# Residual products spread over the norms, high products first, at the boundaries between the calls of a two-block fp32 transformer

## The chip, the cores and the metric

One core of one Trainium2 chip runs the whole program in one launch. The metric is the device time in microseconds; a program's figure is the median of its runs.

## The reference

Two blocks of two layers each work on x, 256 tokens of 1024 channels, in fp32. The first block has attention with context and a Fourier mixer; the second has an RWKV-7 and an mLSTM mixer. What the change touches is the skeleton around them:

```python
# first block, each layer
x_mid = x + g1 * rmsnorm(mix, norm_post_mix[i])
hf = modulate(rmsnorm(x_mid, norm_pre_ffn[i]), sh2, sc2)
x = x_mid + g2 * rmsnorm(swiglu(hf, w_gate[i], w_up[i], w_down[i]), norm_post_ffn[i])
...
# second block, each layer
h = h + HALF * _swiglu(_rmsnorm(h, ffn1_norm[l]), ffn1_w_in[l], ffn1_w_out[l])
xn = _rmsnorm(h, mix_norm[l])
z = xn @ w_in[l]
...
h = h + u @ w_out[l]
h = h + HALF * _swiglu(_rmsnorm(h, ffn2_norm[l]), ffn2_w_in[l], ffn2_w_out[l])
```

`rmsnorm` is x / sqrt(mean(x²) + 1e-6) times a gain, and `modulate` is h(1 + scale) + shift.

## The kernel before

Channels lie on the 128 partitions, so x is 8 blocks (`KD`) of 128 x 256. Weights stream from memory through two-slot rings (`ring_a`, `ring_d`), 1 MB or 0.5 MB at a time. The large products are exact to about fp32 in three reduced-precision (fp32r) products: each operand is split into a high part (a rounding copy) and a low part (the rest), and hi·hi + hi·lo + lo·hi are summed in PSUM (`split_product`, lines 2030 to 2032).

Each engine has its own program, and semaphores join them. There is no scheduler: the order on each engine is the order of the code.

- **TensorE** (`block.tensor`): a norm is `norm_sums` (column sums of the squares, line 2000), `norm_tokens` (line 2009) and `norm_spread` (the inverse root onto all partitions, line 2018). A feed-forward call (`ffn`, seven of them, calls 0 to 6, 22 tiles each) alternates a gate and up tile (`wide_gate_up`, lines 2048 and 2050) with a down tile. In `wide_gate_up` the high and the low part of h stand side by side in `h_parts`, so that one 512-column matmul takes both. Calls 3 to 6 accumulate 2x into the down banks first (lines 2098 to 2103): eight *residual products* of the constant `twice` with a block of x, each two matmul records since it is plain fp32. The sum of 2x and the down product, halved, is the new x.
- **ScalarE**: the norms' squares (`norm`, `norm_squares`, lines 638 and 644), the row copy (662) and the square root (669), the weights' high parts (`round_a`, line 679; `round_d`; t_hi, line 1012), the high parts of h (`round_h`, line 694, with modulation 697 and 698), the evictions and the activations.
- **VectorE**: the reciprocal (`inverse`, 1277), the scaling by the norm (`norm_split`, 1349 and 1351), the weights' low parts (`rest_a`, 1330; `rest_t`, 1608), the halving into x (`half_to_x`, 1587), the addition onto x (1291).
- **GpSimd**: the eight low parts of h (`rest_h`, line 563), and most of the mixer's weight low parts (585).

A boundary between calls is then: squares, sums, row copy, token sums, root, reciprocal, spread, scaling, high parts, low parts, first tile. In TensorE's code all residual products stand between the spread and the first tile, and the first tile's block k waits for the low part of block k (`split_here`). At the first block's second layer ScalarE's `norm` rounds the first weights ahead of the squares of x. The other calls in question are ffn1, mixer and ffn2 of the second block's two layers.

## Time and profile before

| | us |
|---|---|
| median of 3 runs (2487.69 to 2493.08) | 2489.09 |
| the profiled execution's own time | 2488.33 |
| its span in the profile | 2485.8 |
| TensorE busy | 2369.6 (95%) |
| VectorE busy | 1449.3 (58%) |
| ScalarE busy | 1047.2 (42%) |
| GpSimd busy | 319.3 (13%) |

The mean granted clock of TensorE is 0.98 of 2.4 GHz. TensorE's busy time counts a matmul as busy at either clock, so a stretch at 1.2 GHz does not show as idle. The chain that ended last goes through TensorE for 82% of the span. The other engines' busy times are therefore of interest only where TensorE waits for them, and what follows looks there.

### The profile page before, as it was taken

To read this page: it belongs to the slowest core of one execution; us is meant where nothing else is said; L and a number is where in the kernel's file an instruction comes from. 1 tells how busy PE (TensorE), PEld (TensorE's weight loads), DVE (VectorE), ACT (ScalarE), POOL (GpSimd) and SP (SyncE) were. 2 spreads that over 40 slices of the span, in tenths; PEclk is the share of its full clock that TensorE was granted. 3 is DMA by queue.
4 is the path that set the end of the run, shared out by engine and by line. 5 is a ranking of instruction groups with operands and counts; after the bars stand their busy time and mean duration, and the time that the engine had idled before them with its cause. 6 is when DMAs were issued, how large, how long until landed. Compare 5 with 4: busy or idle time off the path is not lost.

```text
span 2485.8 us, 47529 instructions
## 1 busy us (share of the span) xinstructions
PE 2369.6 (95%) x19164; PEld 2095.1 (84%) x19164; DVE 1449.3 (58%) x2314; ACT 1047.2 (42%) x1666; POOL 319.3 (13%) x263
## 2 busy tenths in 40 slices
PE   7988999999998799999999999999999999999998
PEld 3755899999985599879988888899899888988997
DVE  1053266656625276676667765566666668555665
ACT  3154454454335343343346434433433355435333
POOL 0000000000000000010014435300100125336000
PEclk9999999999999899999999999999999999999999
DMA  6255454544425454355433223654455232124542
GB/s 267 71 198 216 178 191 176 189 169 176 169 85 219 154 203 179 150 178 190 177 106 123 81 72 125 220 189 177 154 189 190 102 138 100 69 87 178 201 179 102
DMA packets 65512, 392.51 MB, mean 158 GB/s; under 512 B 7264, under 2 KB 7392, under 8 KB 28000
## 3 DMA queue, kind: packets, MB, share of 16 engines
q1 hardware_dynamic: 64224, 383.81, 42.3%
q10 hardware_dynamic: 864, 5.16, 0.5%
q8 instruction: 104, 1.70, 0.3%
...
HBM read 389.46 MB, written 1.05 MB: 157 GB/s over the span
## 4 chain that ended last, share of the span: by engine, by line
PE 82%; DVE 4%; POOL 4%; issue 4%; ACT 3%; DMA 2%; POOLq 0%; SPq 0%; DVEq 0%; ACTq 0%
PE ps L2048 19%; PE ps L2030 11%; PE ps L2031 11%; PE ps L2032 11%; PE ps L2050 10%; PE ps L2139 6%; POOL t_lo L585 3%; PE ps L2154 2%; PE ps L2453 2%; DMA ring_a<-in_wa 2%; PE ps L2594 1%; POOL h_parts L563 1%; PE ps L2000 1%; PE ps L1977 1%; PE ps L2169 1%
## 5 line engine op out<-in xcount | busy, mean ns | idle before, releaser
L2048 PE MATMUL ps<-h_parts,w_hi 128*128 128x512 f32 x2080 | 742.1, 399 | 4.8 <-DVE mod L1258 2.9
L2050 PE MATMUL ps<-h_parts,w_lo 128*128 128x256 f32 x2080 | 584.9, 281 | 0.0
L2048 PEld LDWEIGHTS ps<-h_parts,w_hi 128*128 128x128 f32 x2080 | 391.9, 188 | 96.7 <-DVE mod L1258 3.2
L2050 PEld LDWEIGHTS ps<-h_parts,w_lo 128*128 128x128 f32 x2080 | 394.1, 189 | 0.1
L1330 DVE TENSOR_TENSOR w_lo<-ring_a,w_hi 128x1024 fp32r<-128x1024 f32 x308 | 366.5, 1232 | 24.7 <-ACT w_hi L679 24.5
L2030 PE MATMUL ps<-hid_hi,d_hi 128*128 128x256 f32 x1232 | 349.0, 283 | 0.0
L2031 PE MATMUL ps<-hid_lo,d_hi 128*128 128x256 f32 x1232 | 348.8, 283 | 0.0
L2032 PE MATMUL ps<-hid_hi,d_lo 128*128 128x256 f32 x1232 | 348.6, 283 | 0.0
L711 ACT ACTIVATE sg<-sg 128x256 f32<-128x256 f32 x130 | 54.3, 418 | 655.5 <-DVE sg L1366 655.5
L679 ACT CAST w_hi<-ring_a 128x1024 fp32r<-128x1024 f32 x308 | 305.6, 1040 | 12.3 <-DMA ring_a<-in_wa 12.3
L2030 PE MATMUL ps<-h_parts,t_hi 128*128 128x256 f32 x880 | 260.8, 296 | 17.4 <-POOL t_lo L585 10.6
L1366 DVE TENSOR_REDUCE sg<-ps 128x256 f32<-128x512 f32 x130 | 89.9, 692 | 302.4 <-PE ps L2050 302.4
L2031 PE MATMUL ps<-h_parts,t_hi 128*128 128x256 f32 x880 | 252.8, 287 | 0.0
L2032 PE MATMUL ps<-h_parts,t_lo 128*128 128x256 f32 x880 | 252.5, 287 | 0.0
L563 POOL TENSOR_TENSOR h_parts<-nsq,h_parts 128x256 fp32r<-128x256 f32 x72 | 61.4, 876 | 1435.1 <-ACT h_parts L698 849.3
L2030 PEld LDWEIGHTS ps<-hid_hi,d_hi 128*128 128x128 f32 x1232 | 234.2, 190 | 6.0
L2032 PEld LDWEIGHTS ps<-hid_hi,d_lo 128*128 128x128 f32 x1232 | 234.6, 190 | 0.0
L2031 PEld LDWEIGHTS ps<-hid_lo,d_hi 128*128 128x128 f32 x1232 | 234.5, 190 | 0.0
L585 POOL TENSOR_TENSOR t_lo<-ring_a,t_hi 128x512 fp32r<-128x512 f32 x120 | 172.7, 1463 | 314.6 <-ACT t_hi L1012 314.6
L1337 DVE TENSOR_TENSOR d_lo<-ring_d,d_hi 128x1024 fp32r<-128x1024 f32 x154 | 190.1, 1235 | 11.5 <-ACT d_hi L687 8.9
L2030 PEld LDWEIGHTS ps<-h_parts,t_hi 128*128 128x128 f32 x880 | 172.2, 196 | 25.9 <-issue 13.6
L2031 PEld LDWEIGHTS ps<-h_parts,t_hi 128*128 128x128 f32 x880 | 173.0, 197 | 0.1
...
## 6 DMA issues: line engine op xcount, KB each, us to landing
...
c<-in_c ACTq DMA_DIRECT2D x1, 1175.0 KB, 10.8
...
```

Of the source, the lines that this page charges most:

```text
L563: nc.gpsimd.tensor_tensor(h_lo[:, k, :], nsq[:, k, :], h_hi[:, k, :].bitcast(F32), ALU.subtract)\
L585: nc.gpsimd.tensor_tensor(t_lo[:, t % 2, k], ring_a[:, c % 2, t % 2, k], t_hi[:, t % 2, k].bitcast(F32), ALU.subtract).then_inc(done, 1)
L679: nc.scalar.copy(w_hi[:, f % 2, part], ring_a[:, c % 2, part]).then_inc(hi_a, 1)
L1330: ins = nc.vector.tensor_tensor(w_lo[:, f % 2, part], ring_a[:, c % 2, part], w_hi[:, f % 2, part].bitcast(F32), ALU.subtract)
L1337: nc.vector.tensor_tensor(d_lo[:, f % 2], ring_d[:, d % 2], d_hi[:, f % 2].bitcast(F32), ALU.subtract)\
L1366: nc.vector.reduce_sum(sg[:, f % 2, :], both_parts(bank), AX_X).then_inc(gate_summed, 1)
L2030: nc.tensor.matmul(out, hi, to_hi, start=start, stop=False, skip_group_check=True)
L2031: nc.tensor.matmul(out, hi, to_lo, start=False, stop=False, skip_group_check=True)
L2032: return nc.tensor.matmul(out, lo, to_hi, start=False, stop=stop, skip_group_check=True)
L2048: nc.tensor.matmul(out, w_hi[:, f % 2, part, k, :], h_parts[:, k], start=(k == 0), stop=False, skip_group_check=True)
L2050: mm = nc.tensor.matmul(out[:, 1, :], w_lo[:, f % 2, part, k, :], h_hi[:, k, :], start=False, stop=(k == KD - 1), skip_group_check=True)
L2139: mm = nc.tensor.matmul(ps[:, 4 + p % 2, 0:cols.stop - cols.start], ring_a[:, slot, i % 2, k, :], h[:, k, cols], start=(k == 0), stop=(k = ...
```

## The change

It does six things.

1. The eight residual products leave the place ahead of the first tile. `norm_residual` puts them between the pieces of the sums, before the token sums, before the spread and behind it, and `ffn(..., last=...)` puts some between tile 0 and tile 1. Each waits for its own piece of x.
2. The first gate and up tile of calls 2 to 6 (`first_gate_up`) and the mixer's first weight tile (`first_tile`) make all products with h's high part first, then those with its low part. The 512-column matmul becomes two of 256 columns.
3. Of h's low parts GpSimd makes five, and VectorE three behind its scaling (both `rest_h`). This holds for calls 2 to 6 and both mixers.
4. In the first block's second layer the squares of the first norm go between the evictions of the projection, the squares of x ahead of the first weights' rounding, which is cut in two, and VectorE writes the modulated h itself (`norm_modulated`) where ScalarE wrote it before.
5. VectorE makes the low part of the first weights earlier (before `half_to_x`) ahead of call 5, and tile 0's low part before `half_to_x` in the mixers.
6. Two turns of the modulation's rows stand ahead of the norm's sums instead of around them.

```diff
...
-                for k in range(KD):
+                for k in range(KD if sid < SHARED else POOL_REST):
                     pool.wait_ge(hh_ready, sid * KD + k + 1)
+                    if sid == SHARED:
+                        pool.wait_ge(h_whole, k + 1)
                     nc.gpsimd.tensor_tensor(h_lo[:, k, :], nsq[:, k, :], h_hi[:, k, :].bitcast(F32), ALU.subtract)\
...
-                        nc.scalar.activation(nsq[:, k, :], hn[:, k, :], ACT.Identity, scale=gains(k), bias=shift(k))
+                        if sid < SHARED:
...
                 modulated = lambda which: (gain_of(l, 2, which), shift_of(l, 3, which))
                 for j in range(KD):
                     empty(f"out1{l}", j, lat[:, j, :])
-                    if l == 0 and j % 2:
+                    if j % 2:
                         if j == 1:
-                            nc.scalar.activation(warm[:, 2:3], const("one"), ACT.Sqrt)
-                        act.wait_ge(proj_free, tile0["out10"] + j + 1)
+                            at = n_id[("post_mix", l, 0)]
+                            nc.scalar.activation(warm[:, at:at + 1], const("one"), ACT.Sqrt)
+                        act.wait_ge(proj_free, tile0[f"out1{l}"] + j + 1)
                         norm_squares(lat, None, [j // 2])
...
                 else:
-                    act.wait_ge(proj_free, tile0[f"out1{l}"] + KD)
-                    norm(("post_mix", l, 0), lat)
-                    g0, g1 = fill(f"M{l}0")
-                    ada(g0)
-                    norm(("pre_ffn", l, 0), x[:, :, :], 2, onto=("post_mix", l, 0), also=lambda: ada(g1))
+                    norm_rows(("post_mix", l, 0))
+                    norm_root(("post_mix", l, 0))
+                    for g in fill(f"M{l}0"):
+                        ada(g)
+                    norm_squares(x[:, :, :], ("post_mix", l, 0))
+                    norm_rows(("pre_ffn", l, 0))
+                    round_a(2, 0, parts=[0])
+                    norm_root(("pre_ffn", l, 0))
+                    round_a(2, 0, parts=[1])
                     round_h(split_id[("pre_ffn", l, 0)], modulated(0))
                     ffn(2)
...
 
-            def norm_split(key, src, call=None, gains=None):
-
-                n, sid = n_id[key], split_id[key]
+            def rest_h(key):
+
+                sid = split_id[key]
+                for k in range(POOL_REST, KD):
+                    dve.wait_ge(hh_ready, sid * KD + k + 1)
+                    nc.vector.tensor_tensor(h_lo[:, k, :], nsq[:, k, :], h_hi[:, k, :].bitcast(F32), ALU.subtract)\
+                        .then_inc(hl_tail if k < KD - 1 else norm_out, 1)
+
+            def norm_split(key, src, call, gains):
+
                 if call is not None:
                     rest_a(call, 0)
                 inverse(key)
-                dve.wait_ge(norm_all, n + 1)
+                dve.wait_ge(norm_all, n_id[key] + 1)
                 for k in range(KD):
-                    if gains is None:
-                        ins = nc.vector.tensor_tensor(hn[:, k, :], src[:, k, :], rstd_of(key), ALU.mult)
-                    else:
-                        ins = nc.vector.scalar_tensor_tensor(nsq[:, k, :], src[:, k, :], gains(k), rstd_of(key),
-                                                             ALU.mult, ALU.mult)
-                    ins.then_inc(v_ready, 1)
+                    nc.vector.scalar_tensor_tensor(nsq[:, k, :], src[:, k, :], gains(k), rstd_of(key),
+                                                   ALU.mult, ALU.mult).then_inc(v_ready, 1)
+                rest_h(key)
+
+            def norm_modulated(key, src, call, gains, shift):
+
+                inverse(key)
+                rest_a(call, 0)
+                dve.wait_ge(norm_all, n_id[key] + 1)
+                for k in range(KD + 1):
+                    if k < KD:
+                        nc.vector.tensor_tensor(hn[:, k, :], src[:, k, :], rstd_of(key), ALU.mult).then_inc(v_ready, 1)
+                    if k:
+                        dve.wait_ge(v_ready, split_id[key] * KD + k)
+                        nc.vector.tensor_scalar(nsq[:, k - 1, :], hn[:, k - 1, :], gains(k - 1), shift(k - 1),
+                                                ALU.mult, ALU.add).then_inc(h_whole, 1)
+                dve.wait_ge(h_whole, KD)
+                rest_h(key)
 
             def ffn(call, beside=None):
...
             dve.wait_ge(norm_out, n_id[("post_ffn", 1, 0)] + 1)
             for l in range(LAYERS):
-                norm_split(("ffn1", l, 0), x, 3 + 2 * l, per_channel("ffn1", l))
+                norm_split(("ffn1", l, 0), x, None if l else 3, per_channel("ffn1", l))
                 ffn(3 + 2 * l)
-                half_to_x(("mix", l, 0))
                 p0 = l * NT2
 
                 def rest_t(t):
@@ -1609,6 +1641,7 @@
                                                 t_hi[:, t % 2, k].bitcast(F32), ALU.subtract).then_inc(done, 1)
 
                 rest_t(0)
+                half_to_x(("mix", l, 0))
...
                 ffn(4 + 2 * l)
+                if l + 1 < LAYERS:
+                    rest_a(5 + 2 * l, 0)
                 half_to_x(("ffn1", l + 1, 0) if l + 1 < LAYERS else ("final", 0, 0))
...
+            def norm_sums(key, before=None):
...
                 for k in range(KD):
+                    if before is not None and k % (KD // PIECES) == 0:
+                        before(k * PIECES // KD)
                     strip = slice(k % STRIPS * STRIP, (k % STRIPS + 1) * STRIP)
                     pe.wait_ge(norm_sq, PIECES * n + k * PIECES // KD + 1)
...
                 norm_tokens(key)
                 norm_spread(key)
 
+            def residual(call, ns):
+
+                for n in ns:
+                    piece = n * PIECES // KD
+                    if call > 3:
+                        pe.wait_ge(resid, PIECES * (3 * ((call - 3) // 2) + (call - 3) % 2 * 2 - 1) + piece + 1)
+                    elif piece < PIECES - 1:
+                        pe.wait_ge(onto_part, (PIECES - 1) * onto_id[("post_ffn", 1, 0)] + piece + 1)
+                    else:
+                        pe.wait_ge(norm_out, n_id[("post_ffn", 1, 0)] + 1)
+                    nc.tensor.matmul(ps[:, n // 2, n % 2 * T:n % 2 * T + T], const("twice"), x[:, n, :],
+                                     start=(n % 2 == 0), stop=False, skip_group_check=True)
+
+            def norm_residual(key, call, pieces, tokens, spread, after):
+
+                norm_sums(key, lambda i: residual(call, pieces[i]))
+                residual(call, tokens)
+                norm_tokens(key)
+                residual(call, spread)
+                norm_spread(key)
+                residual(call, after)
+
             def split_product(out, parts, start, stop):
 
                 hi, lo, to_hi, to_lo = parts
@@ -2033,16 +2092,41 @@
 
             def split_here(key, k):
 
-                if k < KD - 1:
-                    pe.wait_ge(hl_ready, split_id[key] * (KD - 1) + k + 1)
+                sid = split_id[key]
+                if k == KD - 1:
+                    pe.wait_ge(norm_out, n_id[key] + 1)
+                elif sid < SHARED or k < POOL_REST:
+                    pe.wait_ge(hl_ready, pool_rests(sid) + k + 1)
                 else:
-                    pe.wait_ge(norm_out, n_id[key] + 1)
+                    pe.wait_ge(hl_tail, (sid - SHARED) * (KD - 1 - POOL_REST) + k - POOL_REST + 1)
+
+            def hi_here(key, k):
+                pe.wait_ge(hh_ready, split_id[key] * KD + k + 1)
+
+            def first_gate_up(key):
+
+                def out(part, half):
+                    return ps[:, gate_up_bank(0) + part, half * T:half * T + T]
+
+                for k in range(KD):
+                    hi_here(key, k)
+                    for part in range(2):
+                        nc.tensor.matmul(out(part, 0), w_hi[:, 0, part, k, :], h_hi[:, k, :], start=(k == 0),
+                                         stop=False, skip_group_check=True)
+                        nc.tensor.matmul(out(part, 1), w_lo[:, 0, part, k, :], h_hi[:, k, :], start=False,
+                                         stop=False, skip_group_check=True)
+                for k in range(KD):
+                    split_here(key, k)
+                    for part in range(2):
+                        mm = nc.tensor.matmul(out(part, 1), w_hi[:, 0, part, k, :], h_lo[:, k, :], start=False,
+                                              stop=(k == KD - 1), skip_group_check=True)
+                return mm
 
             def wide_gate_up(key, f):
 
+                if f == 0:
+                    return first_gate_up(key)
                 for k in range(KD):
-                    if f == 0:
-                        split_here(key, k)
                     for part in range(2):
                         out = ps[:, gate_up_bank(f) + part, :].rearrange("p (a t) -> p a t", t=T)
...
 
-                if call >= 3:
-
-                    pe.wait_ge(norm_out, n_id[("post_ffn", 1, 0)] + 1)
-                    pe.wait_ge(resid, PIECES * (3 * ((call - 3) // 2) + (call - 3) % 2 * 2))
-                    for n in range(KD):
-                        nc.tensor.matmul(ps[:, n // 2, n % 2 * T:n % 2 * T + T], const("twice"), x[:, n, :],
-                                         start=(n % 2 == 0), stop=False, skip_group_check=True)
                 gate_up(0)
+                residual(call, last)
                 gate_up(1)
                 if call == 1:
...
             for l in range(LAYERS):
-                norm(("ffn1", l, 0))
-                ffn(3 + 2 * l, ("ffn1", l, 0))
+                if l == 0:
+                    norm_residual(("ffn1", l, 0), 3, [(), (0, 1), (2, 3), (4, 5)], (6,), (7,), ())
+                    ffn(3, ("ffn1", l, 0))
+                else:
+                    norm_residual(("ffn1", l, 0), 5, [(), (), (), ()], (0,), (1,), (2, 3, 4))
+                    ffn(5, ("ffn1", l, 0), last=(5, 6, 7))
                 norm(("mix", l, 0))
...
                     wait(pe, t_free, p0 + t - 1, i, 4)
+                    if t == 0:
+                        first_tile(ps[:, bank, 0:T]).then_inc(t_done, 1)
+                        return
                     for k in range(KD):
-                        if t == 0:
-                            split_here(("mix", l, 0), k)
...
                     mm.then_inc(b_done, 1)
-                norm(("ffn2", l, 0))
-                ffn(4 + 2 * l, ("ffn2", l, 0))
+                norm_residual(("ffn2", l, 0), 4 + 2 * l, [(), (), (), (0, 1)], (2,), (3,), (4, 5))
+                ffn(4 + 2 * l, ("ffn2", l, 0), last=(6, 7))
```

The mixer's `first_tile` follows `first_gate_up` with one weight tile in place of two: 16 products with the high part, then 8 with the low part. On TensorE, between the norm in front of call 3 and its first tile (`x,c` is the residual product, `nsq,c` a sum of squares, `c,nrt` the token sums, `c,nst` the spread), there stood before:

```order
L2000 MATMUL ps<-nsq,c 32x256 x8
L2009 MATMUL ps<-c,nrt 128x1 x2
L2018 MATMUL ps<-c,nst 128x128 x2
L2102 MATMUL ps<-x,c 128x256 x8
L2048 MATMUL ps<-h_parts,w_hi 128x512
L2050 MATMUL ps<-h_parts,w_lo 128x256
```

and now stand:

```order
L2037 MATMUL ps<-nsq,c 32x256 x2
L2074 MATMUL ps<-x,c 128x256 x2
L2037 MATMUL ps<-nsq,c 32x256 x2
L2074 MATMUL ps<-x,c 128x256 x2
L2037 MATMUL ps<-nsq,c 32x256 x2
L2074 MATMUL ps<-x,c 128x256 x2
L2037 MATMUL ps<-nsq,c 32x256 x2
L2074 MATMUL ps<-x,c 128x256
L2046 MATMUL ps<-c,nrt 128x1 x2
L2074 MATMUL ps<-x,c 128x256
L2055 MATMUL ps<-c,nst 128x128 x2
L2114 MATMUL ps<-h_parts,w_hi 128x256
```

All eight residual products have moved ahead of the spread. For calls 4 and 6 the places are: two before the last piece of sums, one before the token sums, one before the spread, two behind it, two between tile 0 and tile 1; for call 5 one, one, three and three.

On VectorE, ahead of call 2 in the first block's second layer (`work` is the normalised x in one place and the mix in the other, `mod` the modulation), there stood before:

```order
L1291 TENSOR_TENSOR x<-x,work 128x512 x2
L1258 TENSOR_TENSOR mod<-ps,vec 128x4
L1330 TENSOR_TENSOR w_lo<-ring_a,w_hi 128x1024 x2
L1277 RECIPROCAL nst<-nst 128x2
L1349 TENSOR_TENSOR work<-x,ps 128x256 x8
L1258 TENSOR_TENSOR mod<-ps,vec 128x4
L1269 SCALAR_TENSOR_TENSOR gain<-mod,vec 128x16
L1330 TENSOR_TENSOR w_lo<-ring_a,w_hi 128x1024 x2
```

and now stand:

```order
L1292 RECIPROCAL nst<-nst 128x2
L1345 TENSOR_TENSOR w_lo<-ring_a,w_hi 128x1024 x2
L1381 TENSOR_TENSOR work<-x,ps 128x256 x2
L1384 TENSOR_SCALAR nsq<-work,gain,mod 128x256
...
L1381 TENSOR_TENSOR work<-x,ps 128x256
L1384 TENSOR_SCALAR nsq<-work,gain,mod 128x256 x2
L1360 TENSOR_TENSOR h_parts<-nsq,h_parts 128x256 x3
L1284 SCALAR_TENSOR_TENSOR gain<-mod,vec 128x16
L1345 TENSOR_TENSOR w_lo<-ring_a,w_hi 128x1024 x2
```

The first weights' low pair has moved behind the reciprocal, each of the eight scalings has a modulation behind it, and three low parts of h stand ahead of the second weights' low pair.

## Rows read from the trace of the kernel before

**Rows 1.** The page, first part: busy us, share of the span, records.
```profile
PE 2369.6 (95%) x19164; PEld 2095.1 (84%) x19164; DVE 1449.3 (58%) x2314; ACT 1047.2 (42%) x1666; POOL 319.3 (13%) x263
```

**Rows 2.** Windows (stretch, length, busy us and records per engine, clock, DMA share, GB/s).
```profile
837.00:871.00 34.00, 19.30 (x121) 13.26 (x122) 14.46 (x30) 21.66 (x40) 5.88 (x8) 0.75 0.41 155
1260.00:1278.00 18.00, 14.84 (x89) 12.99 (x88) 11.44 (x21) 8.15 (x17) 6.47 (x8) 0.72 0.17 60
1570.00:1585.00 15.00, 13.28 (x80) 10.38 (x79) 12.02 (x17) 8.54 (x15) 8.07 (x9) 1.00 0.55 211
```

**Rows 3.** Timeline ahead of call 2, A (start, us, engine, line, operation, idle before, releaser).
```profile
839.58 2.09 PE L2000 MATMUL ps<-nsq,c 128*32 128x256 f32 x16 [2.59 <-ACT nsq L638]
...
848.46 1.29 DVE L1291 TENSOR_TENSOR x<-x,work 128x512 f32<-128x512 f32 x2
...
850.07 1.99 ACT L679 CAST w_hi<-ring_a 128x1024 fp32r<-128x1024 f32 x2 [4.45 <-DMA ring_a<-in_wa]
851.97 2.19 ACT L638 ACTIVATE nsq<-x 128x512 f32<-128x512 f32 x4
...
857.62 1.22 PE L2018 MATMUL ps<-c,nst 128*128 128x128 f32 x4 [0.55 <-DVE nst L1277]
...
870.77 0.50 PE L2048 MATMUL ps<-h_parts,w_hi 128*128 128x512 f32 x1 [1.31 <-DVE w_lo L1330]
```

**Rows 4.** Groups by line and form (busy us, mean ns, idle before, releaser).
```profile
L1330 DVE TENSOR_TENSOR w_lo<-ring_a,w_hi 128x1024 fp32r<-128x1024 f32 x308 | 366.5, 1232 | 24.7 <-ACT w_hi L679 24.5
...
L563 POOL TENSOR_TENSOR h_parts<-nsq,h_parts 128x256 fp32r<-128x256 f32 x72 | 61.4, 876 | 1435.1 <-ACT h_parts L698 849.3 <-ACT h_parts L694 585.7
...
L1631 DVE TENSOR_SCALAR work<-work,vec 128x256 f32<-128x256 f32 x8 | 2.3, 349 | 0.1
```

**Rows 5.** Timeline ahead of call 3, B.
```profile
1061.33 1.07 PE L2000 MATMUL ps<-nsq,c 128*32 128x256 f32 x4 [3.10 <-ACT nsq L638]
1062.62 1.07 PE L2000 MATMUL ps<-nsq,c 128*32 128x256 f32 x4 [0.22 <-ACT nsq L638]
...
1067.71 1.22 PE L2018 MATMUL ps<-c,nst 128*128 128x128 f32 x4 [0.55 <-DVE nst L1277]
...
1078.71 0.39 PE L2048 MATMUL ps<-h_parts,w_hi 128*128 128x512 f32 x1
...
1068.97 3.22 DVE L1351 SCALAR_TENSOR_TENSOR nsq<-x,vec,ps 128x256 f32<-128x256 f32 x8 [1.32 <-PE ps L2018]
1073.62 3.33 DVE L1330 TENSOR_TENSOR w_lo<-ring_a,w_hi 128x1024 fp32r<-128x1024 f32 x2 [1.42 <-ACT w_hi L679]
...
1069.49 3.15 ACT L694 CAST h_parts<-nsq 128x256 fp32r<-128x256 f32 x8 [2.03 <-DVE nsq L1351]
...
1069.98 7.56 POOL L563 TENSOR_TENSOR h_parts<-nsq,h_parts 128x256 fp32r<-128x256 f32 x8 [5.28 <-ACT h_parts L694]
```

**Rows 6.** Timeline ahead of layer 0's mixer, C.
```profile
1263.79 0.71 PE L2018 MATMUL ps<-c,nst 128*128 128x128 f32 x4 [0.62 <-DVE nst L1277]
...
1269.18 2.23 DVE L1608 TENSOR_TENSOR t_lo<-ring_a,t_hi 128x512 fp32r<-128x512 f32 x2 [1.42 <-ACT t_hi L1012]
...
1277.09 0.39 ACT L1028 ACTIVATE work<-ps 128x256 f32<-128x256 f32 x1 [2.61 <-PE ps L2032]
```

**Rows 7.** Timeline of TensorE ahead of call 4, D.
```profile
1571.77 0.63 PE L2000 MATMUL ps<-nsq,c 128*32 128x256 f32 x4 [0.46 <-ACT nsq L638]
...
1574.02 0.71 PE L2018 MATMUL ps<-c,nst 128*128 128x128 f32 x4 [0.55 <-DVE nst L1277]
1574.57 3.62 PE L2102 MATMUL ps<-x,c 128*128 128x256 f32 x16
...
1584.18 0.40 PE L2048 MATMUL ps<-h_parts,w_hi 128*128 128x512 f32 x1
```

**Rows 8.** Timeline of TensorE ahead of call 5, E.
```profile
1770.66 1.22 PE L2018 MATMUL ps<-c,nst 128*128 128x128 f32 x4 [1.83 <-DVE nst L1277]
...
1781.76 0.39 PE L2048 MATMUL ps<-h_parts,w_hi 128*128 128x512 f32 x1
```

36 lines of the change are left out of this document (27 added, 9 removed).

## The prediction

> **What bounds the kernel now.** I read the page first: TensorE is busy 95% of the span, 2369.6 us over 19164 matmul records [rows 1]. That is 0.124 us a record, so I take 0.12 us for a 256-column matmul in a stream. Time can only come off where TensorE does not stream, and the change touches seven such places, the boundaries between calls. I name them in order of time: A (before call 2), B (call 3), C (mixer of layer 0), D (call 4), E (call 5), F (mixer of layer 1), G (call 6). The windows around them show what is there [rows 2]: in 34 us around A TensorE is busy 19.3 us at a granted clock of 0.75 of full speed, around C 14.8 of 18 us at 0.72, around D 13.3 of 15 us at 1.00. Many of these boundaries cost twice: holes, and work at 1.2 GHz behind the holes. Then I read each boundary in the timeline. I measure from the end of the norm's spread (the scale factors' matmul) to the start of the next dense tile.
>
> In B the spread ends at 1067.71 + 1.22 = 1068.93, and the second gate and up tile starts at 1078.71, 9.8 us later. Between them, counted from the spread's end: VectorE scales to 3.3 us, ScalarE rounds the high parts from 0.6 to 3.7 us, GpSimd makes the eight low parts from 1.05 to 8.6 us, and VectorE needs 4.7 to 8.0 us for the next weights' low part [rows 5]. So GpSimd is the limiter, and the residual products that stand ahead of the first tile (16 records, 3.62 us at full clock, 0.45 us each of eight [rows 7]) lie mostly beside it. In D the same distance is 1584.18 - 1574.73 = 9.45 us [rows 7], in E 1781.76 - 1771.88 = 9.9 us [rows 8]. In C tile 0 and tile 1 are over at 1277.09, 12.6 us behind the spread's end at 1264.50 [rows 6].
>
> **The common part of the change.** High products no longer wait for GpSimd: they start with the first rounded block at 1.0 us and follow it. 32 of them at 0.12 us take 3.9 us, to 4.9 us; 16 low products add 1.9, to 6.8 us. GpSimd keeps five blocks; at 0.88 us a block (the mean of [rows 4]) they end at 5.4 us. VectorE takes three behind its scaling at 3.3 us. No row shows such a block on VectorE: the low bound is 0.35 us (a 128x256 tensor-scalar [rows 4]), the high bound is 1.2 us, GpSimd's mean block 0.88 plus 0.35 of its own. I take 0.7, between them, because the w_lo pair beside GpSimd took 3.33 us [rows 5] where two at 1.232 us would take 2.46 [rows 4]: the two engines do hold each other up. So VectorE is free at 3.3 + 2.1 = 5.4, and the w_lo pair of the next weights, now alone, ends at 5.4 + 2.4 = 7.8 us. That sets the second tile; the bounds give 6.8 (the low products) and 9.3. The Trainium skill, "SBUF — State Buffer", section "SBUF: two separate sides", says that such a pair of instructions takes an exclusive lock for its whole length, so that one engine fully waits. By it the three blocks of 0.35 us could stand behind two whole GpSimd blocks, 3.3 + 1.05 + 1.76 + 2.4 = 8.5 us, 0.7 worse than my value at each place, about 5 us over all seven; without any contention it would be 6.8 us, up to 7 us better over all. The stretched pair agrees with the direction.
>
> **Boundaries D and G.** Two residuals stand before the last piece of the sums, where TensorE now waits 0.46 us [rows 7]; they take 0.9, so the norm slips 0.45, say 0.5 us. The next two fit into the waits of about 0.5 us for the row copy and the reciprocal (0.55 in [rows 7]). Two more fit ahead of the first rounded block, and the last two between tile 0 (6.8) and 7.8. Gain 9.45 - 7.8 - 0.5 = **1.15 us each, 2.3 together** (bounds -0.4 and 1.8 each). G repeats D.
>
> **Boundary E.** The weights' low pair moves ahead of the half-scaling of x, and the reciprocal stops waiting for it: it delays the spread by 1.83 - 0.55 = 1.3 us now [rows 7, 8], and the spread itself runs 0.5 us longer at half clock (1.22 against 0.71). I take 1.8. The new price is that the half-scaling starts 1 us later; the square roots hide that. Behind the spread come three residuals (1.35 us, 0.35 beyond the hole) and three more behind the first tile: 6.8 + 0.3 + 1.3 = 8.4, which is later than 7.8 and sets the time. Gain 1.8 + 9.9 - 8.4 = **3.3 us** (2 to 4).
>
> **Boundary B.** Here the residuals are a risk. The sums wait for x, piece by piece (3.10 us before the first [rows 5]), and the clock is at half: four records take 1.07 us against 0.63 [rows 5, 7]. Two residuals, four records, cost 0.9 us at full clock and 1.7 at half, three times; the pieces' sums start 1.3 us apart now, with waits of 0.22 us between. So TensorE sets the norm. At half clock until the third pair its end slips by 3.2 us and gets back 0.9, because the steps behind the sums then run at full clock (the spread alone 0.71 us against 1.22 [rows 5, 7]): 2.3 later. If the denser work brings the clock back after the first pair it ends 0.5 later. The common part gives 9.8 - 7.8 = 2.0. So the boundary is worth between -0.3 and +1.5; I take **0.5 us**.
>
> **Boundaries C and F.** The same split, with one weight tile: 16 high products, 8 low ones. Tile 1's first low half would be ready when VectorE is free (5.4) plus half of a pair of 0.65 us, 6.05. At full clock its 24 records end at 8.95, 3.6 us earlier than 12.6; if the clock stays at half as long as now, 1.3 us earlier. I take **2.8 us each, 5.6 together**, between these and nearer the first, since TensorE has fewer gaps there. VectorE's t_lo pair (2.23 us beside GpSimd [rows 6]) loses its companion, which is the reason it is not later. Moving tile 0's low part ahead of the half-scaling costs nothing: the reciprocal is waited for by ScalarE's root either way. F repeats C.
>
> **Boundary A** has three parts. (1) The squares of the first norm are made between the projection's evictions, their table load too. Sums end at 841.67 now; only the last piece (0.63 of square, 0.4 of sums) is left behind the last eviction at 837.4, so they end at 838.6: 3.1 us. (2) The squares of x wait behind the weights' rounding, which waits for its DMA until 850.07; they start at 851.97, though x was complete at 849.75 [rows 3]. Now they go first, as x comes, and the rounding goes into the norm's waits. With x complete 3.1 us earlier, at 846.65: squares done at 847.3, sums 848.0, root 849.8, spread 851.2 at half clock instead of 858.84. The price is on VectorE: the low pair now stands between reciprocal and scaling, to 852.5. (3) ScalarE makes one rounding a block in place of two; VectorE makes the whole part with a tensor-scalar of 0.35 us [rows 4] behind each scaling. A scaling takes 3.22 / 8 = 0.40 us in B [rows 5]: eight rounds of 0.75, to 858.5 (1.1 each if every round waits for GpSimd). Then three low blocks and the gains (1.8 us, to 860.3) and the low pair, 2.4: 862.7, or 863.0 with the waits between. The second tile started at 870.77 [rows 3]. Gain **7.8 us** (bounds 5.3 with each block held up and half clock, 9 without). No DMA is late: the weights' load is released by the ada products, which also come 3.1 us earlier.
>
> **The sum**: 7.8 + 0.5 + 2.8 + 1.15 + 3.3 + 2.8 + 1.15 = 19.5 us. All tiles behind a boundary are TensorE's own time, so I let nothing be given back. The profiled execution took 2488.33 us (span 2485.8) and would take 2468.8. The median of the runs shown is 0.8 us above it; I say 2469.
>
> **Rivals.** (a) *Holes that are no holes*: residuals delay the norms by their full length, as when ScalarE's and VectorE's replies come sooner than a residual ends. Against it stand the waits of 0.46 to 0.55 us beside 0.45. It would take 1.3 us each from D and G, 0.9 from E, 2 from B, 5.5 in all: 2474. (b) *The half clock stays* through the new, denser starts: C and F give 1.3 each, B -0.3, A 5.3, E 2.3, D and G as forecast: 12.2 in all, 2476. For it speaks that before it stayed down through tile 0 and into tile 1 at C. (c) *VectorE becomes the chain*: its three blocks take 1.7 us each behind GpSimd. Then the second tile starts at 3.3 + 5.1 + 2.4 = 10.8: D and G lose 1.85 each, B 2.3, E gains 0.9, C and F lose 0.2 each, A keeps 4: 1.5 us slower, 2490. (d) *Slower: new drops of the clock.* The drops of before fall on stretches where TensorE waits anyway. If the changed rhythm brought a drop of some 10 us (as long as the half-clock stretch that I see behind C) onto dense tiles, half of it is lost, 5.1 us. With one at each of seven boundaries that is 36 - 19.5 = 16 slower, 2505; it decides from four such drops on. Against it: D has none, and the holes get shorter. The Trainium skill, "TensorE: Matmul & The Clock Gate", section "Part 1: The HAM clock gate (the "warmup" mystery)", says that an idle array loses its clock and a busy one gets it back, which speaks against (d).
>
> **How the numbers follow.** Forecast 0.74 (own range 2463 to 2476, from the bounds of A, B and the common part), (a) 0.09, (b) 0.10, (c) 0.04, (d) 0.03. The range is 2462 to 2480: it takes in (a) and (b) and a few us for the spread of the median. A measurement here tells 0.2%, 5 us, from no change. The first three cases are faster by more, 0.93; (c) is within it, 0.04; (d) slower, 0.03.
>
> **What would show it.** Right: the residual line's records spread over the norms; the second tile 7.5 to 8.5 us behind each spread; the spread at A 7.6 us earlier, its second tile 7.8; VectorE's three low blocks at 0.5 to 0.9 us. Wrong: a clock below 0.9 around D or G; sums at B that end more than 2 us later; w_lo of the second weights past 9 us. If the boundaries shrink and the span doesn't, something behind them gave the time back.

## The result, and the profile after

The changed kernel takes 2470.15 us (median of 4 runs, 2469.92 to 2472.8), the kernel before beside it 2491.09 us (4 runs, 2487.69 to 2493.79). The ratio is 0.9918, 95% interval 0.9904 to 0.9932. The forecast was 2469. When the changed kernel ran again beside the experiments below it took 2467.91 us, ratio 0.9919 (0.99 to 0.9939).

The page's first part, of the changed kernel's profiled execution (2472.8 us, span 2471.0):

```profile
PE 2367.2 (96%) x19244; PEld 2093.0 (85%) x19244; DVE 1455.8 (59%) x2343; ACT 1043.9 (42%) x1657; POOL 299.5 (12%) x242
```

Against [rows 1] TensorE is busy 2.4 us less with 80 records more: 512-column matmuls were cut in two. The time came out of its idle time. The windows around A, C and D (columns as in [rows 2], each window moved with its place):

```profile
833.00:867.00 34.00, 27.37 (x174) 20.73 (x173) 19.96 (x41) 17.16 (x29) 3.67 (x5) 0.85 0.51 186
1254.00:1272.00 18.00, 15.69 (x118) 14.13 (x117) 14.39 (x28) 9.87 (x20) 3.69 (x5) 0.91 0.16 58
1561.00:1576.00 15.00, 14.28 (x100) 11.23 (x98) 12.33 (x20) 8.72 (x16) 6.02 (x6) 1.00 0.63 240
```

Against [rows 2], TensorE is busy 8 us more of the 34 at A and its clock is 0.85 instead of 0.75; at C the clock is 0.91 instead of 0.72. GpSimd's eight blocks are five. D stays at full clock. (A window at A that starts with the last eviction, at 840.24, has the same 27.37 us and 0.85.)

The timeline at A, for TensorE, ScalarE, VectorE and GpSimd in turn:

```profile
840.13 1.82 PE L2037 MATMUL ps<-nsq,c 128*32 128x256 f32 x16
...
853.22 0.71 PE L2055 MATMUL ps<-c,nst 128*128 128x128 f32 x4 [0.77 <-DVE nst L1292]
...
866.20 0.50 PE L2132 MATMUL ps<-h_parts,w_hi 128*128 128x512 f32 x1 [0.98 <-DVE w_lo L1345]
...
847.86 1.15 ACT L667 ACTIVATE nsq<-x 128x512 f32<-128x512 f32 x2
...
856.00 0.41 DVE L1384 TENSOR_SCALAR nsq<-work,gain,mod 128x256 f32<-128x256 f32 x1
856.32 0.41 DVE L1381 TENSOR_TENSOR work<-x,ps 128x256 f32<-128x256 f32 x1
856.65 0.78 DVE L1384 TENSOR_SCALAR nsq<-work,gain,mod 128x256 f32<-128x256 f32 x1
...
862.57 1.10 DVE L1360 TENSOR_TENSOR h_parts<-nsq,h_parts 128x256 fp32r<-128x256 f32 x3
...
856.56 0.73 POOL L572 TENSOR_TENSOR h_parts<-nsq,h_parts 128x256 fp32r<-128x256 f32 x1 [356.76 <-DVE nsq L1384]
```

The first norm's sums come directly behind the last eviction (they end at 841.95; the last eviction started at 840.24). The squares of x (L667) start at 847.86, before x is complete. The spread ends at 853.93 (858.84 before), and the second gate and up tile starts at 866.20 (870.77 before [rows 3]). The starts alone hide one thing: the last eviction ahead of A, in code the change does not touch, was 3.2 us later in this profile (837.03 before). Measured from there, the gain at A is 7.8 us. The section on the hardware tells what is known of the 3.2 us.

The timeline at B (TensorE, VectorE, GpSimd):

```profile
1056.84 1.07 PE L2037 MATMUL ps<-nsq,c 128*32 128x256 f32 x4 [3.10 <-ACT nsq L647]
1057.84 2.07 PE L2074 MATMUL ps<-x,c 128*128 128x256 f32 x4
1059.84 0.62 PE L2037 MATMUL ps<-nsq,c 128*32 128x256 f32 x4
...
1065.33 0.71 PE L2055 MATMUL ps<-c,nst 128*128 128x128 f32 x4
...
1073.77 0.50 PE L2132 MATMUL ps<-h_parts,w_hi 128*128 128x512 f32 x1 [0.65 <-DVE w_lo L1345]
...
1069.22 2.22 DVE L1360 TENSOR_TENSOR h_parts<-nsq,h_parts 128x256 fp32r<-128x256 f32 x3
1071.37 2.35 DVE L1345 TENSOR_TENSOR w_lo<-ring_a,w_hi 128x1024 fp32r<-128x1024 f32 x2
...
1067.09 3.73 POOL L572 TENSOR_TENSOR h_parts<-nsq,h_parts 128x256 fp32r<-128x256 f32 x5 [6.87 <-ACT h_parts L703]
```

Two residuals (L2074) took 2.07 us at half clock; behind them the clock was full. The norm, from the first sums to the spread's end, became 1.6 us longer (9.20 against 7.60 from [rows 5]), and the second tile starts 7.7 us behind the spread instead of 9.8: 0.46 us gained.

When the changed kernel ran again, its profile showed B otherwise (TensorE):

```profile
1049.82 2.08 PE L2074 MATMUL ps<-x,c 128*128 128x256 f32 x4
...
1052.83 2.08 PE L2074 MATMUL ps<-x,c 128*128 128x256 f32 x4
...
1058.85 0.71 PE L2055 MATMUL ps<-c,nst 128*128 128x128 f32 x4
```

Four residuals ran at half clock there, the norm took 10.73 us, and B lost 1.05 us.

At C, one of TensorE's high products and ScalarE's second eviction:

```profile
1261.55 0.41 PE L2449 MATMUL ps<-h_parts,t_lo 128*128 128x256 f32 x1
...
1268.95 0.39 ACT L1043 ACTIVATE work<-ps 128x256 f32<-128x256 f32 x1 [1.98 <-PE ps L2091]
```

The spread ends at 1259.76, so the two tiles are over 9.2 us behind it, not 12.6 [rows 6]: 3.4 us. F shows the same 3.4.

The timeline at D (TensorE, VectorE, GpSimd):

```profile
1565.72 0.71 PE L2055 MATMUL ps<-c,nst 128*128 128x128 f32 x4
...
1573.03 1.22 PE L2121 MATMUL ps<-h_parts,w_hi 128*128 128x256 f32 x8 [0.47 <-POOL h_parts L572]
1574.08 1.02 PE L2074 MATMUL ps<-x,c 128*128 128x256 f32 x4
1574.75 0.58 PE L2132 MATMUL ps<-h_parts,w_hi 128*128 128x512 f32 x1
...
1569.61 1.09 DVE L1360 TENSOR_TENSOR h_parts<-nsq,h_parts 128x256 fp32r<-128x256 f32 x3
1571.11 2.94 DVE L1345 TENSOR_TENSOR w_lo<-ring_a,w_hi 128x1024 fp32r<-128x1024 f32 x2 [0.42 <-ACT w_hi L688]
...
1567.46 5.51 POOL L572 TENSOR_TENSOR h_parts<-nsq,h_parts 128x256 fp32r<-128x256 f32 x5 [8.03 <-ACT h_parts L703]
```

The norm ends 0.55 us later than before relative to its first sums, and the second tile is 8.3 us behind the spread, not 9.45 [rows 7]: 0.58 us. At E (below, TensorE) the spread comes at once, where it waited 1.83 us [rows 8], and the second tile follows 8.8 us behind it; G gained 0.54 us.

```profile
1760.20 0.71 PE L2055 MATMUL ps<-c,nst 128*128 128x128 f32 x4
...
1769.67 0.58 PE L2132 MATMUL ps<-h_parts,w_hi 128*128 128x512 f32 x1
```

Groups by line and form (busy us, mean ns, idle before):

```profile
L572 POOL TENSOR_TENSOR h_parts<-nsq,h_parts 128x256 fp32r<-128x256 f32 x51 | 41.9, 841 | 1436.3 <-ACT h_parts L703 591.4 <-ACT h_parts L708 486.9 <-DVE nsq L1384 357.9
...
L1360 DVE TENSOR_TENSOR h_parts<-nsq,h_parts 128x256 fp32r<-128x256 f32 x21 | 12.0, 626 | 0.0
```

GpSimd makes 51 blocks of 841 ns where it made 72 of 876 [rows 4]; VectorE makes 21 at 626 ns.

Together the seven places gave 7.8 + 0.5 + 3.4 + 0.6 + 2.85 + 3.4 + 0.5 = 19.0 us. Read in the same way, the second profile of the changed kernel gives 7.1 - 1.05 + 3.1 + 0.6 + 3.6 + 3.4 + 0.8 = 17.5 us.

### The profile page after: what moved, and what is told of

The parts are those of the page before. It is cut to its first block, busy times and chain, and to the rows that moved or that the text cites. A ratio compares the mean times of both kernels' runs of the same rounds, so it can differ in the third digit from the quotient of the medians.

```text
span 2471.0 us, 47691 instructions
## 1 busy us (share of the span) xinstructions
PE 2367.2 (96%) x19244; PEld 2093.0 (85%) x19244; DVE 1455.8 (59%) x2343; ACT 1043.9 (42%) x1657; POOL 299.5 (12%) x242
## 3 DMA queue, kind: packets, MB, share of 16 engines
HBM read 389.46 MB, written 1.05 MB: 158 GB/s over the span
## 4 chain that ended last, share of the span: by engine, by line
PE 83%; DVE 5%; issue 4%; POOL 3%; DMA 2%; ACT 2%; SPq 0%; POOLq 0%; DVEq 0%; ACTq 0%
PE ps L2132 19%; PE ps L2089 11%; PE ps L2090 11%; PE ps L2091 11%; PE ps L2134 10%; PE ps L2217 6%; POOL t_lo L594 3%; PE ps L2232 2%; PE ps L2552 2%; DMA ring_a<-in_wa 1%; PE ps L2693 1%; PE ps L2037 1%; PE ps L2012 1%; PE ps L2247 1%; DMA work<-in_wa 1%
## 5 line engine op out<-in xcount | busy, mean ns | idle before, releaser
L2132 PE MATMUL ps<-h_parts,w_hi 128*128 128x512 f32 x2000 | 712.0, 399 | 1.6 <-DVE w_lo L1345 1.6
L2134 PE MATMUL ps<-h_parts,w_lo 128*128 128x256 f32 x2000 | 561.6, 281 | 0.0
L2132 PEld LDWEIGHTS ps<-h_parts,w_hi 128*128 128x128 f32 x2000 | 376.0, 188 | 89.3 <-DVE w_lo L1345 2.0
L2134 PEld LDWEIGHTS ps<-h_parts,w_lo 128*128 128x128 f32 x2000 | 378.0, 189 | 0.1
L1345 DVE TENSOR_TENSOR w_lo<-ring_a,w_hi 128x1024 fp32r<-128x1024 f32 x308 | 363.8, 1223 | 13.4 <-ACT w_hi L688 13.2
L2089 PE MATMUL ps<-h_parts,t_hi 128*128 128x256 f32 x864 | 252.6, 292 | 15.8 <-POOL t_lo L594 13.1
L2090 PE MATMUL ps<-h_parts,t_hi 128*128 128x256 f32 x864 | 246.1, 285 | 0.0
L2091 PE MATMUL ps<-h_parts,t_lo 128*128 128x256 f32 x864 | 245.8, 285 | 0.0
L572 POOL TENSOR_TENSOR h_parts<-nsq,h_parts 128x256 fp32r<-128x256 f32 x51 | 41.9, 841 | 1436.3 <-ACT h_parts L703 591.4
L2089 PEld LDWEIGHTS ps<-h_parts,t_hi 128*128 128x128 f32 x864 | 167.3, 194 | 22.9 <-issue 14.5
L696 ACT CAST d_hi<-ring_d 128x1024 fp32r<-128x1024 f32 x154 | 161.0, 1045 | 25.6 <-PE ps L2091 25.4
```

The costliest lines, as they stand in the source:

```text
L696: nc.scalar.copy(d_hi[:, f % 2], ring_d[:, d % 2]).then_inc(hi_d, 1)
L1345: ins = nc.vector.tensor_tensor(w_lo[:, f % 2, part], ring_a[:, c % 2, part], w_hi[:, f % 2, part].bitcast(F32), ALU.subtract)
L2089: nc.tensor.matmul(out, hi, to_hi, start=start, stop=False, skip_group_check=True)
L2090: nc.tensor.matmul(out, hi, to_lo, start=False, stop=False, skip_group_check=True)
L2091: return nc.tensor.matmul(out, lo, to_hi, start=False, stop=stop, skip_group_check=True)
L2132: nc.tensor.matmul(out, w_hi[:, f % 2, part, k, :], h_parts[:, k], start=(k == 0), stop=False, skip_group_check=True)
```

## The experiments

Ten more kernels ran, and the changed one once more. For each I give its whole time and, from its profile, the **sum over the boundaries**: at each of the seven places the time from a point ahead of the norm (the last eviction at A, the first sums elsewhere) to the first product of the first down projection, at the mixers to the second tile's eviction. This sum leaves out what the clock does in the rest of the program. Because it ends later than the second tile's start, it gives the change 18.2 us in the first profile and 16.6 in the second. The ratios are taken to runs of the kernel before beside each kernel (their medians were 2488.10, 2488.86 and 2487.58 us), so they compare better than the medians do.

| kernel | median us | ratio (interval) | boundaries us |
|---|---|---|---|
| before | 2489.09 | 1 | 154.8 |
| changed | 2470.15 | 0.9918 (0.9904 to 0.9932) | 136.6 |
| changed, again | 2467.91 | 0.9919 (0.99 to 0.9939) | 138.2 |
| residuals behind the norm | 2467.95 | 0.9915 (0.989 to 0.994) | 138.5 |
| all low blocks on GpSimd | 2482.54 | 0.9989 (0.9974 to 1.0005) | 153.4 |
| A undone | 2479.33 | 0.9964 (0.9947 to 0.998) | 145.0 |
| products interleaved | 2474.25 | 0.9941 (0.9923 to 0.9958) | 138.7 |
| four blocks on GpSimd | 2471.11 | 0.9928 (0.9911 to 0.9946) | 134.4 |
| four blocks, residuals in holes only | 2469.36 | 0.9924 (0.9907 to 0.9942) | 135.1 |
| before, with sharing only | 2485.38 | 0.9989 (0.9978 to 1.0001) | 150.4 |
| weights' order undone | 2472.3 | 0.9936 (0.9918 to 0.9954) | 136.4 |
| A: squares behind | 2474.1 | 0.9944 (0.9925 to 0.9962) | 138.9 |
| A: ScalarE modulates | 2471.41 | 0.993 (0.991 to 0.995) | 138.7 |

The two profiles of the changed kernel differ by 1.6 us in the sum, mostly because the clock fell at other moments within A and B. So I take nothing below 2 us from a sum alone, and read single rows for what is smaller.

### Residuals behind the norm again

```diff
-norm_residual(("ffn1", l, 0), 3, [(), (0, 1), (2, 3), (4, 5)], (6,), (7,), ())
+norm_residual(("ffn1", l, 0), 3, [(), (), (), ()], (), (), range(KD))
-norm_residual(("ffn2", l, 0), 4 + 2 * l, [(), (), (), (0, 1)], (2,), (3,), (4, 5))
+norm_residual(("ffn2", l, 0), 4 + 2 * l, [(), (), (), ()], (), (), range(KD))
```

(Call 5 likewise, and none behind tile 0.)

> The changed kernel with all eight residual products behind the spread again, at boundaries B, D, E and G; all else as changed. Theory (the residuals' new places matter only by what they take off the path to the second tile): 3.6 us of residuals, then 3.9 us of high and 1.9 us of low products put the second tile 9.3 to 9.5 us behind the spread at D, E and G (changed kernel: 8.3, 8.8 and 7.7), while the norms at D and G no longer slip by 0.5 us and B's no longer by 1.6 us. Net: B +1, D +0.5, E +0.5, G +1, together 3 us slower than the changed kernel, about 2473. Rival (the residuals were the whole gain at these four places): 3.6 us each, 14 us slower, 2484. Second rival (their places cost as much as they save): no difference at B, or faster there.

Ratio 0.9915: no slower, so the second rival held and the theory's 3 us are not there. At D, TensorE's spread, the residuals and the second tile:

```profile
1557.90 0.71 PE L2055 MATMUL ps<-c,nst 128*128 128x128 f32 x4 [0.55 <-DVE nst L1292]
1558.44 3.62 PE L2074 MATMUL ps<-x,c 128*128 128x256 f32 x16
...
1567.65 0.40 PE L2132 MATMUL ps<-h_parts,w_hi 128*128 128x512 f32 x1
```

The second tile is 9.0 us behind the spread instead of 8.3, but the norm is 0.54 us shorter: the boundary takes 19.2 us in both. At B the norm is 7.6 us and not 9.2, and the tile behind it 2.5 us later: 0.85 us worse than the changed kernel's first profile, 0.7 us better than its second. Over B, D, E and G together this kernel takes 80.6 us where the changed one takes 79.4 and 79.9. So the residuals' new places, which give the change its name, are worth about 1 us over all by the profiles, less than a sum can tell, and nothing by the median. The theory counted the norm's slip, but put the tile at 9.3 to 9.5 us where it came at 9.04, and G's slip at 0.5 where it is 1.1.

### All low blocks on GpSimd

```diff
-        SHARED = 2
+        SHARED = 99
...
```

VectorE's `rest_h` goes too; what the change does at A stays.

> The changed kernel with GpSimd making all eight low parts of h again at all seven boundaries; high products first and the residuals' places as changed. Theory (the three low parts on VectorE carry the common part of the gain): GpSimd's last block comes 8.6 us behind the spread at B, D, E and G, so the second tile starts 9.0 to 10.4 us behind it: B +1.3, D +1.6, E +1.6, G +2.2, C and F +1.9 each, A +1.5, together 12 us slower than the changed kernel, about 2482. Rival (it is the order of the products that gains, whoever makes the low parts): less than 3 us slower, up to 2473.

Ratio 0.9989 (0.9974 to 1.0005), median 2482.54: almost the whole gain is gone. The theory (12 us slower, 2482) held, and the rival is out. At D, GpSimd, VectorE and the last low products on TensorE:

```profile
1567.21 7.58 POOL L572 TENSOR_TENSOR h_parts<-nsq,h_parts 128x256 fp32r<-128x256 f32 x8 [8.03 <-ACT h_parts L703]
...
1570.86 3.34 DVE L1345 TENSOR_TENSOR w_lo<-ring_a,w_hi 128x1024 fp32r<-128x1024 f32 x2 [1.42 <-ACT w_hi L688]
...
1574.84 0.50 PE L2110 MATMUL ps<-h_parts,w_hi 128*128 128x256 f32 x2 [1.16 <-POOL h_parts L572]
```

GpSimd needs 7.58 us for eight blocks, the w_lo pair runs into it and takes 3.34 us, and TensorE waits 1.16 us for the last block. The boundaries from B to G take 121.8 us. Before the change they took 115.8, with it 105.3. So high products first and residuals in the norm, without the sharing, made the six places 6 us worse: the norms got longer, and the tile behind them still waited for GpSimd. Not all of the 6 us is this: B (3.9) and G (3.0) make more than the whole of it, and G, whose code is D's, took 22.6 us against D's 20.5, at a granted clock of 0.90 behind the spread where D had 1.00.

### Before, with sharing only

The kernel before, and only `rest_h` added: GpSimd five blocks, VectorE three.

> The kernel before with one thing of the change: VectorE makes three of h's eight low parts at all seven boundaries. Everything else as before (interleaved products, residuals ahead of tile 0, A and E in their old order). Theory (the sharing needs its companions at B, D, E and G, because TensorE's own 3.6 us of residuals and 5.7 of products fill 9.4 us there): C and F gain 3.2 us each, B, D, E and G 0 to 0.4 each, A 0 to 0.5: 7 us faster than the kernel before, ratio 0.997. Rival (the sharing carries the common part alone): 2 us at each boundary, 14 us faster, ratio 0.994.

Ratio 0.9989 (0.9978 to 1.0001), boundaries 150.4: less than the theory's 7 us, and the rival's 14 us are out. C gained 2.8 us and F 2.0. At D, TensorE's spread and residuals, VectorE's blocks and pair:

```profile
1579.62 0.71 PE L2052 MATMUL ps<-c,nst 128*128 128x128 f32 x4 [0.55 <-DVE nst L1286]
1580.17 3.62 PE L2071 MATMUL ps<-x,c 128*128 128x256 f32 x16
...
1583.51 2.15 DVE L1354 TENSOR_TENSOR h_parts<-nsq,h_parts 128x256 fp32r<-128x256 f32 x3
1585.58 2.35 DVE L1339 TENSOR_TENSOR w_lo<-ring_a,w_hi 128x1024 fp32r<-128x1024 f32 x2
```

VectorE is done with the pair 7.6 us behind the spread (1587.93 - 1580.33), and TensorE sets the second tile: the eight residuals, 3.62 us, stand ahead of the whole first tile. At D the boundary takes 18.9 us, no more than the 19.2 of the changed kernel. B to G took 111.3 us, 4.5 less than before. Sharing alone gives 4.5, the other parts alone lose 6, both together gain 10.5: **the two halves pay more together than one by one**. The medians say the same: 3.5 us for sharing alone (2488.86 - 2485.38, its interval reaches 1), 12.4 for sharing as the last part put in (2482.54 - 2470.15).

Why they do is only in part shown. That each half removes one of two limits that lie close to each other is what the rows at D suggest, but at D, where all profiles show full clock, the whole change is no better than sharing alone. Some 10 of the 12 us by which the parts fail to add up are at B and G. There the clock differed as well: in the kernel with sharing only the residuals ran at half clock at B (5.7 us, where they took 3.4 at D), and G took 20.5 us where D, with the same code, took 18.9 (clock 0.93 behind the spread against 1.00). At C and E the parts nearly add up.

### A undone

The squares behind the evictions, ScalarE's modulation, and the old order of rounding, squares and modulation turns, all at A alone.

> The changed kernel with boundary A's own parts undone: squares behind all evictions, the weights' rounding ahead of the squares of x, the modulated h written by ScalarE; high products first and VectorE's three low blocks stay at A too. Theory: A gives back 7.3 to 7.8 us (0.5 may stay through the shared low parts), about 2477.5; nothing moves at B to G. Rival (A's gain is an effect of the clock, which differs between executions there): less than 4 us slower.

A grows from 31.3 to 39.1 us, 7.7; the whole is at 0.9964, 9 to 11 us above the changed kernel's medians. The theory (7.3 to 7.8) held at A, and the rival (under 4 us) is out. TensorE at A, the two norms' sums:

```profile
838.51 2.09 PE L2036 MATMUL ps<-nsq,c 128*32 128x256 f32 x16 [2.59 <-ACT nsq L645]
...
851.59 2.54 PE L2036 MATMUL ps<-nsq,c 128*32 128x256 f32 x16 [6.18 <-ACT nsq L645]
```

The waits of 2.59 and 6.18 us for ScalarE's squares are back.

### A, two pieces of it

```diff
-                    if j % 2:
+                    if l == 0 and j % 2:
...
-                    norm_rows(("post_mix", l, 0))
-                    norm_root(("post_mix", l, 0))
+                    act.wait_ge(proj_free, tile0[f"out1{l}"] + KD)
+                    norm(("post_mix", l, 0), lat)
```

Here the first norm's squares follow the last eviction in one piece.

> Of the work ahead of call 2 only this is undone: ScalarE squares the first norm's blocks in one piece behind the last eviction again, and not in pairs between the evictions. It leaves the two residuals, the modulation on VectorE and the low parts shared. My theory: the norms there (last eviction to the end of the second norm's spread) grow from 13.3 to about 16.5 us, nothing changes behind the spread, and the whole is 3 us slower than the changed kernel. Rival: ScalarE is not what the first norm waits for, since VectorE's seven x adds come between as well: then under 1 us.

TensorE's sums at A, waiting for ScalarE's squares:

```profile
837.15 2.09 PE L2037 MATMUL ps<-nsq,c 128*32 128x256 f32 x16 [2.59 <-ACT nsq L647]
```

The norms there grow from 13.32 (14.53 in the second profile) to 17.46 us, 2.9 to 4.1, and the median is at 2474.1. The theory's 3 holds. The rival (under 1 us) is out.

In the other kernel ScalarE writes the modulated block and its high part again, and VectorE only the scaling:

> Of the work ahead of call 2 only this is undone: VectorE writes the eight scaled blocks alone, ScalarE writes the modulated values and their high parts, and GpSimd takes the last low blocks by the count of ScalarE's values, as before. The squares stay between the evictions. My theory: the rounds behind the spread follow ScalarE's two instructions per block again (about 1.3 us a round where VectorE's rounds took 1.03), so the second tile starts 2 to 2.5 us later behind its spread and the whole is about 2 us slower. Rival: the low products (6.8 us at TensorE) bound the second tile in both, and VectorE freed of the modulation makes the low parts sooner: then no change, or up to 1 us faster.

TensorE's second tile, ScalarE's two instructions for one block and its rounding of the next weights, and VectorE's pair of w_lo:

```profile
861.96 0.50 PE L2138 MATMUL ps<-h_parts,w_hi 128*128 128x512 f32 x1 [0.74 <-DVE w_lo L1343]
...
851.53 0.58 ACT L705 ACTIVATE nsq<-work,mod,gain 128x256 f32<-128x256 f32 x1
852.02 0.58 ACT L706 ACTIVATE h_parts<-work,mod,gain 128x256 fp32r<-128x256 f32 x1
...
858.41 1.98 ACT L686 CAST w_hi<-ring_a 128x1024 fp32r<-128x1024 f32 x2
...
859.55 2.36 DVE L1343 TENSOR_TENSOR w_lo<-ring_a,w_hi 128x1024 fp32r<-128x1024 f32 x2 [0.50 <-ACT w_hi L686]
```

The norm is as in the second profile of the changed kernel (14.52), and the second part 1.05 us longer (18.54 against 17.49). ScalarE's two instructions start 0.49 us apart, so its round takes 0.98 us, not the 1.3 that I expected; VectorE's took 1.03. The modulation on VectorE makes no faster rounds. It is worth 1 us because it clears ScalarE: with two instructions a block it rounds the next w_hi only at 858.41, 9.2 us behind the spread (8.0 in the changed kernel's second profile), and VectorE's pair waits 0.50 us for that. Both the theory (2 to 2.5) and the rival (none) missed. Of A's 7.7 us about 3 are the squares between the evictions and 1 is the modulation. The rest, near 3.5, is left for the squares of x ahead of the weights' rounding and the turns of the modulation's rows together. It is known by subtraction only; neither was run alone.

### Products interleaved again

```diff
-                if f == 0:
-                    return first_gate_up(key)
                 for k in range(KD):
+                    if f == 0:
+                        split_here(key, k)
...
```

The mixers' first tile likewise.

> The changed kernel with the products of the first tile interleaved again, block k waiting for its low part; VectorE makes three of them, the residuals stay where the change puts them. Theory (sharing the low parts is what counts, and the order of the products then adds little, because the second tile waits for its own weights' low part at 7.7 us): tile 0 ends 7.6 us behind the spread in place of 6.8, D, E and G lose 0.2 to 0.8 each as their last residuals follow tile 0, B, C and F lose nothing to 0.3, A up to 1: 1 to 3 us slower than the changed kernel, about 2472. Rival (high products first is what gains): 2 us a boundary, 12 us slower or more, 2482.

Boundaries 138.7, only 2.0 more than the changed kernel's first profile and 0.5 more than its second; the whole median lies 4 to 6 us above, with intervals that overlap. The theory (1 to 3 us slower) is nearer than the rival (12), which is out. At D the distance behind the spread was 14.19 us, as in the changed kernel (14.16). Once the low blocks are shared, a product that waits for its low block costs little in the profile. At F it costs more in this profile: the two tiles are over 10.7 us behind the spread instead of 9.2, at a clock of 0.68 (0.82 and 1.00 in the changed kernel's two profiles). The kernel with sharing only, interleaved too, shows the same 10.7 at 0.68, while two kernels with high products first show 9.7 and 9.8 at 0.65. Where the rest of the median's 4 to 6 us lies I can't say from these profiles.

### The weights' order undone

```diff
-                norm_split(("ffn1", l, 0), x, None if l else 3, per_channel("ffn1", l))
+                norm_split(("ffn1", l, 0), x, 3 + 2 * l, per_channel("ffn1", l))
```

At the mixers `half_to_x` comes ahead of t_lo again.

> Only the two moves on VectorE are undone: before call 5 its first pair of w_lo stands between the scale of the first norm and the eight scales again, and at the mixers the half of x comes ahead of t_lo again. My theory: ahead of call 5 the spread comes 1.3 to 1.8 us later (the pair is behind the reciprocal, which is what the spread's last products wait for), nothing at the mixers (their t_lo is bound by the spread and by GpSimd), and the whole is 1 to 2 us slower than the changed kernel. Rival: the move at the mixers carries half of the 3.4 us gained there each; then the first evictions behind the mixers' spreads come 1.5 us later each, and the whole is 4 to 5 us slower.

At E, TensorE's spread, VectorE's pair and its reciprocal:

```profile
1760.22 0.71 PE L2053 MATMUL ps<-c,nst 128*128 128x128 f32 x4 [1.28 <-DVE nst L1292]
...
1757.73 2.36 DVE L1345 TENSOR_TENSOR w_lo<-ring_a,w_hi 128x1024 fp32r<-128x1024 f32 x2
1760.01 0.15 DVE L1292 RECIPROCAL nst<-nst 128x2 f32<-128x2 f32 x1
```

The pair stands ahead of the reciprocal again, the spread waits 1.28 us, and the norm takes 5.08 us against 3.86: 1.2 us. The whole is at 0.9936, 2 to 4 us above, within the intervals. At the mixers the distances are 12.91 and 12.99 us, the changed kernel's 12.93 and 12.97: nothing, as the theory had it, and the rival is out.

### Two attempts to do better

GpSimd with four blocks and VectorE with four (`POOL_REST = 4`); and the same with the residuals at every place as at E, few of them inside the norm.

> The changed kernel with four low parts of h on GpSimd and four on VectorE. Theory (two SBUF readers exclude each other on these two engines, and GpSimd's fifth block is what collides): GpSimd ends 4 us behind the spread, VectorE's four blocks end at 5.2 to 5.5 us in one go, no GpSimd block waits behind a w_lo pair, and the second tile starts 7.6 to 7.8 us behind the spread at B, D and G, 8.4 at E (changed kernel: 7.7, 8.3, 7.7, 8.8): 1 to 1.5 us faster over all. Rival (VectorE is the chain, each block on it costs): 0.4 us slower at each of seven boundaries, 3 us.

> As e5, and at B, D and G the residual products take E's places: none between the sums, one before the token sums, one before the spread, three behind it, three behind tile 0. Theory (residuals between the sums delay the norm by what they take, those in the reply holes and behind the spread do not): B's norm takes 7.6 us in place of 9.2 to 10.7, D's and G's 4.5 in place of 5.0 and 5.7; the second tiles start 8.4 us behind the spread. B 1 to 2.4 us, D 0.3, G 0.4 less than in e5: 2 to 3 us faster than e5, 3 to 4 faster than the changed kernel. Rival (the clock falls at D or G without residuals between the sums): their norms take 5.5 us and more, and nothing is gained.

> The changed kernel itself, unaltered, on this chip beside the next three, as their reference. Theory (the boundaries as read): 18 to 20 us below the kernel before. Its boundary B shows whether the norm there takes 9.2 us or, with the clock at half for longer, 10.7.

The kernel with four blocks did at the places what its theory said (second tiles 7.5 to 7.6 us behind the spread at B, D and G, 8.0 at E), but its median shows none of it. The other one gained nothing over it: D's norm took 4.5 us and G's 4.8, but B's took 8.1, and B's second tile came 9.0 us behind the spread instead of 8.4. The changed kernel, run again, was 20.2 us faster by its ratio, a little over the theory's 18 to 20, and its norm at B took the 10.7 us of the longer half clock.

Both have the shortest boundaries, 134.4 and 135.1 us, but neither is faster than the changed kernel beside them: 0.9928 and 0.9924 against 0.9919, all within their intervals. Two or three microseconds at the boundaries do not show in the whole time here. I would keep the changed kernel.

## Why the prediction was right

**The common part held by its steps at B and G.** VectorE was to be free at 5.4 us behind the spread and done with w_lo at 7.8. In B three blocks took 2.22 us (0.74 each, forecast 0.7) and the pair 2.35 (forecast 2.4): 7.68 us, and the tile started at 7.73; in G at 7.69. TensorE's low products ended at 6.9 to 7.1 (forecast 6.8), so w_lo did set the tile in B. In G the last residuals end at the same moment. Rival (c), VectorE as the chain with 1.7 us a block, is out.

**D and E were forecast 1.15 and 3.3 and gave 0.58 and 2.85.** The norm's slip was right in D (0.55, forecast 0.5). What failed is the term "GpSimd's five blocks end at 5.4": in D and E they took 5.5 us from their start and ended 6.5 us behind the spread, because the fourth block waited beside VectorE's three (it ended at 4.9 us) and the fifth fell behind the first w_lo of the pair. In B and G they ended at 4.8, so 5.4 was right at none of the four. TensorE waited 0.47 us for it, and the residuals came on top: 8.3 in D, 8.8 in E (forecast 7.8 and 8.4). G had the other order and yet gave only 0.54. There the slip of the norm was 1.2 us, since its sums waited once more (0.48) ahead of the residuals.

**B: 0.5 forecast, 0.46 measured**, from a slip of 1.6 (between my 0.5 and 2.3) and 2.05 behind the spread (forecast 2.0). That the number fits is luck of the execution: in the second profile the slip was 3.1, above my upper bound, and B lost 1.05 us. The sums ended 2.5 us later in the first profile and 4.0 in the second, counted from their start, which the prediction had named as a sign of being wrong (more than 2). The step that was too low is the price of the residuals between the sums.

**C and F: 2.8 each forecast, 3.4 measured.** The step was the blend between full clock (3.6) and half clock (1.3). TensorE did its high products at half clock (0.41 us each where full clock gives 0.28) and yet was not what the second tile waited for. So the clock cost almost nothing there, and the upper end was the value to take. In the second profile F ran at full clock throughout and took the same (9.25 us behind the spread against 9.23).

**A: 7.8 forecast, 7.8 measured (7.1 in the second profile), but with two errors against each other.** VectorE's rounds took 1.03 us, not 0.75 (the upper bound of 1.1 was nearer), and all of them 7.2 us instead of 6.0. Against that the spread came 0.5 us earlier than I had it, and the three low blocks with the gains took 1.2 instead of 1.8. The kernel in which ScalarE modulates shows how little the modulation's place decides.

**The whole.** 19.0 us at the places (17.5 in the second profile) against 19.5. In the profiled executions 15.5 of them are seen (2488.33 - 2472.8), because this execution was 3.2 us late ahead of A. The two medians differ by 20.9 us, 2 to 3.5 more than the places give, and no run shows where these come from; that the total is so near is in part luck. Rival (b), that the half clock stays, came true in part (C's and F's high products, B's residuals), but its price did not: C and F gave 3.4; rival (d), new drops onto dense tiles, did not happen at the boundaries of the changed kernel (for drops elsewhere, see the last section). Rival (a), holes that are no holes, was given 5.5 us for the residuals' whole delay. With the residuals taken out of the norms the time stayed the same, so (a) was nearer the truth on the residuals than its chance of 0.09 says, though its time was not. The gain came from sharing together with the products' order, from A, and from the reciprocal's place at E.
